# Where twelve steps of the second half stand against the first expert rows

## The reference

```
mod = silu(c) @ w_ada + b_ada                        # shifts, scales, gates
h = modulate(rms_norm(x, g1), shift1, scale1)
proj = h @ w_in                                      # attention q k v, delta rule q k v z b a
mix = concat([attention, gated delta rule]) @ w_out
x = x + gate1 * mix
h2 = modulate(rms_norm(x, g2), shift2, scale2)
# peer(h2), for each token: 8 heads, 16 experts a head
s1, s2 = query . keys1, query . keys2                # 128 keys each
top 16 of s1, top 16 of s2, top 16 of the 256 sums -> 16 experts of 16384, softmax -> gates
act = gelu(expert_down[e] . h2)
y = sum over 8 * 16 experts of gate * act * expert_up[e]
out = x + gate2 * y
```

## Time and profile before

| | |
|---|---|
| Time, median of 3 runs | 3431.4 us (3430.27 to 3432.34) |
| The profiled execution's own time | 3429.41 us |
| Its span, first to last instruction | 3427.6 us |
| Mean granted clock of PE | 0.953 of full speed |
| PE, DVE, ACT, POOL busy | 2961.7, 2116.6, 1407.3, 647.6 us |
| DMA over the span | 797.82 MB, 232 GB/s read and written in HBM |

### The profile page before, as it was taken

The page is one execution under the profiler, slowest core; times in us unless marked ns, Lnnn a source line. Parts: engine busy times, 40 slices in busy tenths (PEclk is TensorE's granted clock), DMA queues, the critical chain, the costliest instruction groups (busy, mean ns, idle before and its releaser), DMA issues.

```text
span 3427.6 us, 34615 instructions
## 1 busy us (share of the span) xinstructions
PE 2961.7 (86%) x12002; PEld 2061.8 (60%) x12002; DVE 2116.6 (62%) x3960; ACT 1407.3 (41%) x2884; POOL 647.6 (19%) x572
## 2 busy tenths in 40 slices
PE   6989999899877989998998797887879777777777
PEld 5868888687655768886777663565547332223222
DVE  7664443686556354432452879879768979655555
ACT  3243222444555342223652256773433433333333
POOL 0000000000110000000000022334543444443442
PEclk9999999999899999999999999999989899999999
DMA  6534444243111424442311478988999899999998
GB/s 250 185 130 142 147 139 145 92 147 99 50 50 50 146 94 147 142 145 89 106 55 62 172 283 306 349 351 355 406 420 418 350 421 421 421 422 421 422 421 339
DMA packets 147549, 797.82 MB, mean 233 GB/s; under 512 B 16305, under 2 KB 18481, under 8 KB 81713
## 3 DMA queue, kind: packets, MB, share of 16 engines
q0 software_dynamic: 73728, 536.90, 38.6%
q1 hardware_dynamic: 69840, 251.69, 22.2%
q10 hardware_dynamic: 3808, 7.02, 0.6%
HBM read 793.46 MB, written 2.10 MB: 232 GB/s over the span
## 4 chain that ended last, share of the span: by engine, by line
PE 50%; DMA 20%; DVE 18%; ACT 8%; issue 4%; POOL 0%; DVEq 0%; SPq 0%; POOLq 0%; ACTq 0%
PE psum L153 50%; DMA tail<-in_experts,tail 19%; DVE tail L187 4%; ACT L164 3%; ACT arena L164 2%; DVE tail L170 2%; DVE tail L182 2%; DVE region L170 1%; DVE tail L193 1%; DVE arena L182 1%; ACT tail L164 1%; DVE tail L190 1%; DVE rounded L170 1%; DVE tail L196 1%; DVE tail L205 1%
## 5 line engine op out<-in xcount | busy, mean ns | idle before, releaser
L153 PE MATMUL psum<-tail,arena 128*128 128x256 f32 (+2 forms) x3580 | 1274.8, 505 | 262.2 <-ACT arena L164 231.0
L153 PE MATMUL psum<-rounded,rounded 128*128 128x512 f32 x5496 | 1280.0, 393 | 31.8 <-DVE rounded L182 22.6
L153 PEld LDWEIGHTS psum<-rounded,rounded 128*128 128x128 f32 x5496 | 1035.5, 190 | 253.2 <-issue 31.7
L153 PEld LDWEIGHTS psum<-tail,arena 128*128 128x128 f32 x3580 | 676.2, 199 | 813.8 <-issue 755.0
L216 POOL DMA_INDIRECT tail<-in_experts,tail x512 | 585.8, 1144 | 1227.6 <-PE psum L153 763.0
L187 DVE CUSTOM_DVE_ANT_0 tail<-tail 128x1024 f32<-128x1024 f32 x512 | 621.2, 1223 | 314.4 <-DMA tail<-in_experts,tail 312.1
L164 ACT ACTIVATE tail<-tail 128x1 f32<-128x1 f32 (+1 forms) x1056 | 266.3, 252 | 772.3 <-DVE tail L187 735.1
L170 DVE TENSOR_TENSOR rounded<-arena,rounded 128x1024 fp32r<-128x1024 f32 (+2 forms) x285 | 316.5, 1111 | 365.8 <-ACT rounded L164 365.6
L164 ACT ACTIVATE rounded<-arena 128x1024 fp32r<-128x1024 f32 (+2 forms) x317 | 292.0, 939 | 407.9 <-DVE arena L170 232.5
L164 ACT ACTIVATE arena<-psum 128x256 f32<-128x256 f32 (+2 forms) x210 | 97.6, 480 | 409.2 <-PE psum L153 408.4
L170 POOL TENSOR_TENSOR arena<-arena 128x512 f32<-128x512 f32 x32 | 41.7, 1303 | 1153.4 <-ACT arena L164 1153.4
(11 more groups left out here) (85 smaller groups left out, 1521.6 us busy)
## 6 DMA issues: line engine op xcount, KB each, us to landing
arena<-in_ada SPq DMA_DIRECT2D x136, 512.0 KB, 3.7
arena<-in_fin SPq DMA_DIRECT2D x88, 512.0 KB, 4.2
arena<-in_win SPq DMA_DIRECT2D x56, 512.0 KB, 3.3
arena<-in_fout SPq DMA_DIRECT2D x32, 512.0 KB, 4.0
arena<-in_mxbc SPq DMA_DIRECT2D x32, 512.0 KB, 3.8
arena<-in_pq SPq DMA_DIRECT2D x32, 512.0 KB, 7.9
arena<-in_ain SPq DMA_DIRECT2D x24, 512.0 KB, 4.7
arena<-in_mz SPq DMA_DIRECT2D x16, 512.0 KB, 3.3
```

The costliest lines, as they stand in the source:

```text
L153: return self.e.matmul(o, a, b, start=start, stop=stop, skip_group_check=skip)
```

## The change

The twelve steps no longer stand before the first row. `before_rows` only takes the rest of chunk 0's ranking, on ACT and DVE (on PE it isn't called: there it had no ranking to take). `steps_of` gets a second step of the second half in each of chunk 0's first twelve pairs (rows 0 to 23). Behind the twelfth pair both kernels have issued 24 steps of the second half, and from there the lists are the same. No instruction's work is changed.

```diff
--- before.py
+++ after.py
@@ -2372,17 +2372,16 @@
                 e.dma(out[0, 128 * c:128 * c + 128, 512 * u:512 * u + 512], fin_out[:, 512 * u:512 * u + 512]).then_inc(
                     *stored.tick((c, u), u))
 
-        EARLY, LEFT = 12, 12
-
-        def before_rows(main, ranks):
-
-            for i in range(LEFT):
-                some(ranks, 1)
-                if i < EARLY:
-                    some(main, 1)
+        LEFT, TWICE = 12, 12
+
+        def before_rows(ranks):
+
+            some(ranks, LEFT)
 
         def steps_of(c, grp, main, ranks):
 
+            if c == 0 and grp < TWICE:
+                some(main, 1)
             if c < 2 and next(main, True) is None:
                 some(ranks, 1 + grp % 2 if c == 0 else 0)
             else:
@@ -2392,7 +2391,6 @@
 
         def pe_experts(e):
             main = pe_main(e, 1)
-            before_rows(main, iter(()))
             for g, (c, grp) in enumerate(ALL_GROUPS):
                 if grp == 0:
                     ranks = iter(()) if c == 3 else wait_steps(33)
@@ -2410,7 +2408,7 @@
         def act_experts(e, ranks):
             ranked = [ranks] + [act_topk(e, c) for c in range(1, 4)]
             main = act_main(e, 1, ranked[2])
-            before_rows(main, ranks)
+            before_rows(ranks)
             for g, (c, grp) in enumerate(ALL_GROUPS):
                 if grp == 0:
                     ranks = iter(()) if c == 3 else ranked[c + 1]
```

## The result

The changed kernel takes 3437.57 us (median of 18 runs, 3431.11 to 3440.68), the kernel before on the same chips 3431.91 (18 runs): a ratio of 1.0016 with a 95% interval of 1.0009 to 1.0022. It is 5.7 us slower, clear of noise but under the 0.2% of the prediction. The forecast was 3435, +3.5.

A forecast was written before the change was run, and what follows sets the result against it. PE was taken as the bound to row 19's adding, then DVE; PE's lateness of 9.4, then 6.8 us, left DVE +3.4 at row 24, taken as +3.5 on the median 3431.4: 3434.9, say 3435, range 3421 to 3442.

The forecast's parts named there:

- Part 1: Rows put in front of the twelve steps: row 0 starts on DVE 5.8 us sooner, with one more 1.28 us table load.
- Part 2: Norm's steps 0 to 7 inside the first four pairs: first projection at 1997.1 against 1973.88, PE 9.4 us behind in work.
- upper bound: Low clock through row 7: adds of rows 6 and 7 and a first projection step at half speed, +7, in all +10.
- Part 3: Steps 8 to 19, two projection steps a pair, PE the bound: row 19 added at 2063.5, 6.8 us later.
- Part 4: From there to row 24: PE +4.6 us, DVE +3.4; DVE's number carries, PE's excess goes into slack; +3.5 taken.
- The early start carries: Rival: the rows' stream, not PE, sets row 24; end 17 us sooner, 3414; chance 0.17 for over 6.9 us gain.
- The chain through three engines: Rival: roots between rows on three engines, two steps a pair, stall PE: +10, 3442; chance 0.25 for over 6.9 us.
- No trace of it: Rival: the shift is lost in later stretches or the lists don't differ in effect: 3431.4; no separate chance given.
- lower bound: Sum of PE's work from 1971 with PE never idle: row 23 added at 2062.4, 4.4 us sooner than before.

The follow-up runs named there:

- e5: The changed kernel plus matmuls nobody reads on PE: 30 ahead of row 0 and six more before rows 6 and 7 are added; 3435.22 us.
- e1: Against the kernel before: the norm's eight steps stay ahead of row 0, only four projection steps move, one into each of the first four pairs; 3431.77 us.
- e9: Against e8: the four projection steps 8 to 11 go behind the start of the rows, one more in each of the first four pairs; 3426.23 us.
- e8: Against e4: the norm's root one ranking step sooner, still all twelve steps ahead of row 0; 3418.37 us.
- e6: Against e1: the four extra projection steps stand in pairs 4 to 7 instead of pairs 0 to 3; 3432.81 us.
- e4: Against the kernel before: all twelve steps still ahead of row 0, but the norm put inside the last ranking steps; 3422.34 us.
- e3: The changed kernel plus matmuls nobody reads on PE: 30 ahead of row 0 and three more before rows 6 and 7 are added; 3437.31 us.

## Why the prediction was right, and where its size was off

**The sign and the place held.** The bound was put on PE's list up to step 19, then on DVE, and the forecast said that row 24 decides. Row 24's shift and the time agree in all ten kernels, and the difference at row 24 (7.7 in the two profiles) is that at row 504 (7.9). That DVE's number carries and PE's excess goes into slack came true as well: PE's adding of row 23 (gather 30) is 8.5 us later, DVE's dot of row 24 6.3, and the time 5.7.

**Part 1 held.** Row 0 starts 57.0 us behind the first gather, before 63.0: 6.0 sooner, forecast 5.8. The added table load is there, and so is the first sum on PE, 28 us after its last work (the ACT load, DVE's first dot and PE's sum):

```profile
1970.50 1.28 ACT L164 ACT_TABLE_LOAD   x1
...
1971.28 1.22 DVE L187 CUSTOM_DVE_ANT_0 tail<-tail 128x1024 f32<-128x1024 f32 x1
...
1975.32 3.75 PE L153 MATMUL psum<-arena 128*128 128x256 f32 x8 [28.06 <-ACT arena L164]
```

**Part 2 held but for the clock.** Forecast was step 8 at 1997.1, which is 84.2 behind the first gather. Measured 87.1. e5 gives 84.2 once rows 6 and 7 run at the full clock. The prediction had the price (2 x 1.72 on rows 6 and 7) in its upper bound and not in its sum; the other half of that bound, a projection step at half speed, did not come. One remark of this part is off: PE idle for about 8 us. Its own times leave 1997.1 - 1973.9 - 13.8 - 3.4 = 6.0 us; measured are 2.96 us of idle time and about 6 lost to the low clock, on the sums and rows 0, 1, 6 and 7. The rows:

```profile
1984.83 7.04 PE L153 MATMUL psum<-tail,arena 128*128 128x512 f32 x16
1994.83 20.50 PE L153 MATMUL psum<-tail,arena 128*128 128x512 f32 x64 [2.96 <-ACT arena L164]
```

Sixteen matmuls of rows 2 to 5 end near 1992, and the next start at 1994.83 after 2.96 us idle, so the clock was low (0.51 from 1994 to 2001) on work that was on the path. The chain ahead is as written: root on ACT after rows 4 and 5, load, Ln, load, Exp, with 1.29 and 1.30 us from a load to the next ACTIVATE and no drain to be seen:

```profile
1985.64 1.28 ACT L164 ACT_TABLE_LOAD   x1
1986.93 0.47 ACT L164 ACTIVATE arena<-psum,arena 128x256 f32<-128x256 f32 x1
1987.42 1.28 ACT L164 ACT_TABLE_LOAD   x1
1988.72 0.42 ACT L164 ACTIVATE arena<-arena 128x256 f32<-128x256 f32 x1
```

**Part 3 held.** PE is busy 72.0 of 72 us from 1995 to 2067. The adding of row 19 (gather 26) is 9.3 later, forecast 6.8: 2.5 more. With the clock held up (e5) it is 6.3 later, 0.5 less than forecast.

**Part 4 is the term that was mis-sized, by what it inherited.** Forecast +3.5 for row 24, measured +6.3, and +3.4 in e5 with the clock held up. So of the miss of 2.8 us the low clock at rows 6 and 7 is 2.9; the rest of the sum came out within 0.1 us at row 24. That closeness is in part luck: in e5 row 19 is added 0.5 us less late than forecast and row 23 1.0 more (5.6 against 4.6), and the two don't reach DVE's number.

**The rivals.** "The early start carries": fell. Gather 7 is 16.8 us sooner and the time is worse; e1 (gather 7 12 us sooner, time unchanged) and e9 (3.7 sooner than in e8, time worse) show it twice more. "The chain through three engines": its low clock is what came true, at about 3 us; its stalls by roots two steps a pair are worth at most 1.6 us (e6) and not 7. "No trace of it": fell, since the shift stays to the last row and the interval leaves out no change. The lower bound, 4.4 us of gain if PE never idled, was a bound for this order alone: e4 and e8 show that the same twelve steps ahead of the rows give 10 and 13 when the norm doesn't wait for the ranking's Exp. The prediction read the gap of 16.54 us as the shadow of the ranking and did not ask what ended it: it was the order of ACT's and DVE's lists, which held the root and the scaling behind the ranking's last step, and not a need for its result.

## What to carry to other kernels

An engine that stands still is not by itself something to fill: ask which list it will be late with next. Here gathers and dots were brought forward, at most by 12 us in e1 and by 17 in the changed kernel: for nothing where the full engine (PE) kept its work as it was (e1), and at a loss where PE got its next 70 us of work later. Before moving such cheap work up, move up the short cross-engine chain (sum, root, scaling) that releases the full engine's work, and look in every in-order list for an instruction that waits for something else ahead of it. And a short gap ahead of work on the path can cost more than its length: here 2.96 us of waiting brought another 2.9 by the clock.

## What the runs showed of the hardware

What PE's low clock cost here depended on what ran in it. Keeping PE busy for 26 us ahead of row 0 (e3, clock 1.00 to 1994) changed nothing in row 24 or the time; a gap of 2.98 us after that still gave 0.51 from 1994 to 2001, and filling it to 0.41 us gave 1.00 there and brought row 24 2.9 us sooner.
